# Stick-breaking attention: scan pairs counted over all rows of units, and one ScalarE gate for both heads of a step

## The chip, the cores and the metric

The program runs on one NeuronCore of a Trainium2 chip. The metric is device time in microseconds (us), the median of three runs. PE is TensorE's matmul stream and PEld its weight loads, DVE is VectorE, ACT is ScalarE, POOL is GpSimd, SP is SyncE, which here only issues DMAs.

## The reference, cut to what matters

The layer has an input projection, an mLSTM half, a stick-breaking attention half and an output projection over 4096 positions. The change touches the attention half alone, which has 8 heads of 64:

```python
z = q.k / sqrt(d)                                  # for t, s with s < t
A[t, s] = sigmoid(z_ts) * prod_{s<j<t} (1 - sigmoid(z_tj))
out[t] = sum_s A[t, s] v[s]
```

The kernel computes the gates `1 - sigmoid(z)` and their running product from the newest key to the oldest. A telescoped sum then needs only that product and differences of neighbouring values of `v` (the tensor `dw`).

## The kernel before, in words

The stage `stage_attend` works on 4 head pairs one after the other. For a pair of heads it takes the queries in 16 rows of 256 (two halves `i` of 128), from the last row (`cb` = 15) to the first (`cb` = 0). A row walks its keys in chunks of 512 from the diagonal backwards; one row and one chunk are a **unit**. The rows have 8, 8, 7, 7, 6, 6, ..., 1, 1 units, 72 per head pair and 288 in all. Within a head pair I number them 0 to 71: unit 22 is the last of row `cb` = 13, unit 23 the first of row `cb` = 12, units 66 and 67 are row `cb` = 3, 68 and 69 row `cb` = 2, 70 is row `cb` = 1, 71 is row `cb` = 0. "Unit 72" is the first of the next head pair. The first unit of a row holds the diagonal and is narrower: its halves are 384 and 512 columns wide for an odd `cb`, 128 and 256 for an even one.

For each unit:

- `scores(u)`, PE, L1329: z of both halves and both heads into four PSUM banks `a_z`; each of the 12 matmuls is 512 wide at most.
- `gates(u)`, ACT, L1426: the sigmoid from `a_z` into `a_ring`, four instructions (2 halves by 2 heads).
- the mask, POOL, L1305, for a diagonal unit.
- the scan, DVE, L1509: the running product in place in `a_ring`. Two units of a row that follow each other lie side by side in a slot of the ring, and one scan of up to 1024 columns runs over both: four scans (2 halves by 2 heads) for a pair. A row with an odd number of units ends with a pair of one, scanned 512 wide. The scan of a pair starts from the last column of the pair before. The ring has 3 slots.
- `turn(u, 0)` and `turn(u, 1)`, PE, L1345: transposes into `a_rt`, after all four scans of the pair.
- `copies(u, .)`, ACT, L1437 to L1440: `a_rt` to `a_turned`.
- `weigh(u)`, PE, L1358: the product with `dw` into `a_acc`, one unit later; `row_out`, ACT, L1450, empties it at a row's end, and SP stores the row (L1214).

Each engine works through its own fixed list and waits on semaphores. PE's list for a unit is `turn(u, 0)`, the scores of a later unit, `turn(u, 1)`, `weigh(u - 1)`; ACT's is `copies(u, 0)`, the gates of that later unit, `copies(u, 1)`. Which later unit goes by pairs: during pair p the units of pair p + 2 are scored and gated.

SP's list holds, row pair by row pair, the load of queries `a_q` for two groups of rows ahead (L1200), the stores, and the reload of the keys for the next head pair (L1206 to L1209). So the queries of unit 72 are loaded behind the store of unit 65's row and four key loads. For the last head pair two sets of loads for the next stage (L1515 to L1521) stand in that place.

Of the kernel before, what the change touches and what calls it, by code (L numbers as in the profile page):

```python
# [7 lines left out]
ALU = mybir.AluOpType  # L8
ACT = mybir.ActivationFunctionType

P = 128
# [1102 lines left out]
def stage_attend(nc, d, cols, wout_hi, wout_lo, w_out, csil, w_ada, gate_sum, b_ada, g_post, held, mix_in, o_st):  # L1114
# [34 lines left out]
    PAIRS, PAIR_OF = [], []  # L1149
    for row in range(len(LAST)):  # L1150
        for u in range(LAST[row - 1] + 1 if row else 0, LAST[row] + 1, 2):
            PAIRS.append(range(u, min(u + 2, LAST[row] + 1)))
            PAIR_OF += [len(PAIRS) - 1] * len(PAIRS[-1])

    def place(u):
        return PAIR_OF[u] % RP, 1 - (u - PAIRS[PAIR_OF[u]][0])

    with ExitStack() as ctx:
# [18 lines left out]
        z = [ps(f"z{k}", [P, CH]) for k in range(ZB)]  # L1177
# [138 lines left out]
        def _(pe):  # L1316
            def scores(u):
                hp, row, cb, j = UNITS[u]
                g = row // 2
                pe.wait_ge(q_in[g % 2], 32 * (g // 2 + 1))  # L1320
                pe.wait_ge(chunk_in[j], 64 * (hp + 1))
                for i in range(2):
                    at, w = 4 * u + 2 * i, width(u, i)
                    after(pe, keep_done, at + 2 - ZB)
                    t, s = (cb % 2 * 2 + i) * P, slice(j * CH, j * CH + w)
                    for part, (qp, k) in enumerate(((0, khi), (1, khi), (0, klo))):
                        for h in range(2):
                            e = slice(h * SD, (h + 1) * SD)
                            mm = pe.matmul(z[(at + h) % ZB][:, 0:w], q_sb[e, g % 2, qp, t:t + P], k[e, s], start=part == 0, stop=part == 2)  # L1329
                            if part == 2:  # L1330
                                mm.then_inc(z_done, 1)

            def turn(u, pair):
                k = FIRST[u] + pair
                slot, part = place(u)
                pe.wait_ge(scan_done, 4 * PAIR_OF[u] + 4)
# [41 lines left out]
            for u in range(2, PAIRS[1][-1] + 1):  # L1378
                scores(u)
            pe.wait_ge(g_act, 4)  # L1380
            for p, pair_units in enumerate(PAIRS):
                ahead = list(PAIRS[p + 2]) if p + 2 < len(PAIRS) else []
                for u in pair_units:
                    turn(u, 0)
                    if ahead:
                        scores(ahead.pop(0))
                    if blocks(u) > 2:
                        turn(u, 1)
                    if u == pair_units[-1] and ahead:
                        scores(ahead.pop(0))  # L1390
                    if u:
                        weigh(u - 1)
# [3 lines left out]
        def _(act):  # L1396
# [59 lines left out]
            for u in range(2, PAIRS[1][-1] + 1):  # L1456
                gates(u)
            for p, pair_units in enumerate(PAIRS):
                ahead = list(PAIRS[p + 2]) if p + 2 < len(PAIRS) else []
                for u in pair_units:  # L1460
                    if u >= 2:
                        row_out(u - 2)
                    copies(u, 0)
                    if ahead:
                        gates(ahead.pop(0))
                    if blocks(u) > 2:
                        copies(u, 1)
                    if u == pair_units[-1] and ahead:
                        gates(ahead.pop(0))
# [4 lines left out]
        def _(dve):  # L1474
# [21 lines left out]
            for p, pair_units in enumerate(PAIRS):  # L1496
                for s in range(4):
                    head, i = pair_units[0], s // 2
                    run = slice(0 if len(pair_units) == 2 else CH, CH + width(head, i))
                    n = run.stop - run.start  # L1500
                    dve.wait_ge(keep_done, 4 * pair_units[-1] + s + 1)
                    if diag(head):
                        dve.wait_ge(mask_done, 2 * UNITS[head][1] + i + 1)
                        first = 1.0
                    else:
                        dve.wait_ge(scan_done, 4 * p + s + 1 - 4)
                        first = ring[:, (p - 1) % RP, s, 0, 0:1]
                    line = ring[:, p % RP, s].rearrange("p a t -> p (a t)")[:, run][:, ::-1]
                    dve.tensor_tensor_scan(line, line, zeros[:, 0:1].to_broadcast([P, n]), first, ALU.mult, ALU.add).then_inc(scan_done, 1)  # L1509
# [450 lines left out]
```

## Time and profile before

| | |
|---|---|
| median of 3 runs | 3421.31 us (3420.1 to 3422.13) |
| profiled execution, its own time | 3418.25 us |
| its span, first to last instruction | 3416.5 us |
| busy: PE, DVE, ACT, POOL | 3253.6, 2420.9, 1929.0, 849.3 us |
| attention, first to last scan | 1582.4 to about 2878 us |

The busy time of an engine counts its instructions from start to end. Two instructions that follow each other overlap a little, so the distance between two starts, not the duration, says how fast an engine gets on. An idle time in brackets in the timeline stands before the instruction, with what released it. PE may be shown busy while it only advances as fast as its matmuls end.

### The profile page before, as it was taken

What the parts mean: (1) busy time and instruction counts of PE and PEld (TensorE: products, weight loads), DVE (VectorE), ACT (ScalarE), POOL (GpSimd) and SP (SyncE); (2) the same over time, 40 slices, a digit from 0 to 9 for tenths busy, and PEclk for the clock granted to TensorE, in tenths of its full rate; (3) what the DMA queues carried; (4) which work ended last, traced back from release to release, by engine and by line L of the source; (5) the groups of instructions that cost most, each with busy time, mean ns of one, the idle gap of its engine ahead of it and who ended that gap; (6) DMA issues with size and microseconds to landing.
All of it is one profiled execution on the core that took longest, in us unless ns stands there. A gap on an engine that the chain in (4) does not pass through costs nothing. (4 is left out here: it accounts for less than half of the span.)

```text
span 3416.5 us, 72847 instructions
## 1 busy us (share of the span) xinstructions
PE 3253.6 (95%) x28402; PEld 2672.1 (78%) x28402; DVE 2420.9 (71%) x2989; ACT 1929.0 (56%) x4177; POOL 849.3 (25%) x677
## 2 busy tenths in 40 slices
PE   6998999999999999997999999999999998999998
PEld 4776888999999988886776676666667666888887
DVE  4675445443578893325999999999999997666665
ACT  4553123222334452225888888888888886555554
POOL 1323332300000004422123322521252224232322
PEclk8999999999999999998999999999999999999999
DMA  8989778977955579974011201121121013566664
GB/s 293 337 311 327 257 254 308 313 237 239 320 159 189 181 251 320 319 259 139 25 34 58 62 28 44 48 67 31 40 59 50 11 33 97 177 205 200 200 205 135
DMA packets 415600, 582.65 MB, mean 171 GB/s; under 512 B 35568, under 2 KB 298096, under 8 KB 414288
## 3 DMA queue, kind: packets, MB, share of 16 engines
q1 hardware_dynamic: 394560, 506.56, 44.9%
q0 software_dynamic: 16960, 58.73, 5.1%
q10 hardware_dynamic: 3792, 13.30, 1.1%
q8 instruction: 207, 3.39, 0.4%
q14 instruction: 81, 0.66, 0.1%
HBM read 393.74 MB, written 184.75 MB: 169 GB/s over the span
## 5 line engine op out<-in xcount | busy, mean ns | idle before, releaser
L1509 DVE TENSOR_TENSOR_SCAN a_ring<-a_ring,a_zeros 128x1024 f32<-128x1024 f32 (+6 forms) x640 | 1230.9, 1998 | 67.6 <-ACT a_ring L1426 67.6
L1440 ACT COPY a_turned<-a_rt 128x512 f32<-128x512 f32 x960 | 528.3, 618 | 149.9 <-PE a_rt L1345 149.4
L1426 ACT ACTIVATE a_ring<-a_z 128x512 f32<-128x512 f32 (+3 forms) x1152 | 563.2, 602 | 3.4 <-PE a_z L1329 3.4
L1358 PE MATMUL a_acc<-a_turned,c_dw 128*64 128x256 f32 x4352 | 520.6, 380 | 7.0 <-ACT a_osum L1450 7.0
L1345 PEld LDWEIGHTS a_rt<-c_ident,a_ring 64*128 64x128 f32 x8448 | 328.0, 139 | 204.1 <-issue 95.6
L1345 PE MATMUL a_rt<-c_ident,a_ring 64*128 64x64 f32 x8448 | 370.6, 226 | 70.0 <-ACT a_turned L1440 31.6
L1305 POOL TENSOR_SCALAR_AFFINE_SELECT a_ring<-a_ring 128x256 f32<-128x256 f32 x128 | 196.8, 1552 | 893.9 <-ACT a_ring L1426 893.5
L1358 PEld LDWEIGHTS a_acc<-a_turned,c_dw 128*64 128x64 f32 x4352 | 287.4, 137 | 157.6 <-ACT a_turned L1438 9.9
L1329 PE MATMUL a_z<-c_khi,a_q 64*128 64x512 f32 (+3 forms) x2304 | 373.7, 401 | 22.9 <-DMA c_dw<-scratch_dw 12.5
L939 DVE TENSOR_TENSOR p_hlo<-p_wraw,p_hlo 128x1024 fp32r<-128x1024 f32 x85 | 104.5, 1229 | 323.2 <-ACT p_hlo L704 323.2
L704 ACT CAST p_hlo<-p_wraw 128x1024 fp32r<-128x1024 f32 x85 | 89.3, 1050 | 391.5 <-PE p_bank L572 209.5
L1329 PEld LDWEIGHTS a_z<-c_khi,a_q 64*128 64x128 f32 x2304 | 199.9, 190 | 52.3 <-issue 28.3
L1329 PE MATMUL a_z<-c_klo,a_q 64*128 64x512 f32 (+3 forms) x1152 | 224.7, 379 | 0.0
L640 POOL DMA_DIRECT2D p_hraw<-scratch_sbv x32 | 22.7, 715 | 706.5 <-DVE p_ob L1083 617.9
L939 DVE TENSOR_TENSOR p_aslot<-p_wraw,p_aslot 128x1024 fp32r<-128x1024 f32 x43 | 53.7, 1248 | 171.5 <-ACT p_aslot L704 171.3
L704 ACT CAST p_aslot<-p_wraw 128x1024 fp32r<-128x1024 f32 x43 | 45.1, 1050 | 203.3 <-PE p_bank L572 107.1
L572 PE MATMUL p_bank<-p_hhi,p_hlo 128*128 128x512 f32 x528 | 122.9, 390 | 5.2 <-DMA p_hlo<-scratch_parts 5.2
L1329 PEld LDWEIGHTS a_z<-c_klo,a_q 64*128 64x128 f32 x1152 | 113.6, 187 | 17.5
L572 PE MATMUL p_bank<-p_whi,p_hlo 128*128 128x512 f32 x528 | 123.9, 390 | 2.0 <-DMA p_hlo<-scratch_parts 2.0
L580 PE MATMUL p_bank<-p_hlo,p_whi 128*128 128x256 f32 x1008 | 124.5, 283 | 0.0
L580 PE MATMUL p_bank<-p_hlo,p_wlo 128*128 128x256 f32 x1008 | 124.4, 283 | 0.0
L1625 POOL TENSOR_TENSOR m_qs<-c_khi,m_wq 128x512 f32<-128x512 f32 x32 | 41.7, 1302 | 332.6 <-ACT m_wq L1767 328.5
(298 smaller groups left out, 6384.8 us busy)
## 6 DMA issues: line engine op xcount, KB each, us to landing
p_hlo<-scratch_parts SPq DMA_DIRECT2D x130, 512.0 KB, 5.2
p_wraw<-scratch_sums SPq DMA_DIRECT2D x128, 512.0 KB, 6.7
p_aslot<-scratch_parts SPq DMA_DIRECT2D x62, 512.0 KB, 5.0
p_u<-in_w_in POOLq DMA_DIRECT2D x64, 256.0 KB, 6.0
scratch_wsums<-p_u POOLq DMA_DIRECT2D x32, 512.0 KB, 6.5
p_hraw<-scratch_sbv POOLq DMA_DIRECT2D x32, 512.0 KB, 7.2
m_xt<-in_x SPq DMA_DIRECT2D x32, 512.0 KB, 5.1
out_y<-c_pair SPq DMA_DIRECT2D x32, 512.0 KB, 4.5
```

Source lines behind the costliest of these rows:

```text
L572: last = pe.matmul(dst[:], stationary, moving, start=fresh and k == 0 and e == 0, stop=k == 3 and e == 2, skip_group_check=True)
L580: last = pe.matmul(part, stationary, moving, start=fresh and mm == 0 and k == 0 and e == 0, stop=k == 3 and e == 2, skip_group_check=True)
L704: act.copy(a_flat[q % 3][0], araw[k % 2]).then_inc(a_hi, 1)
L939: dve.tensor_tensor(al, araw[k % 2], ah.bitcast(F32), ALU.subtract).then_inc(a_lo, 1)
L1305: pool.affine_select(out=tail, in_=tail, compare_op=ALU.is_gt, fill=1.0, base=0, pattern=[[0, 2], [-1, P]], channel_multiplier=1).then_inc ...
L1329: mm = pe.matmul(z[(at + h) % ZB][:, 0:w], q_sb[e, g % 2, qp, t:t + P], k[e, s], start=part == 0, stop=part == 2)
L1345: last = pe.transpose(rt[(2 * k + half) % RB][:, at:at + HB], ring[rows, slot, 2 * i + h, part, kb * P:(kb + 1) * P], ident[rows, rows])
L1358: last = pe.matmul(acc[h * SD:(h + 1) * SD, lo:QW], dw[:, h, j * TPC + kb, :], turned[:, (FIRST[u] + kb // 2) % TB, kb % 2, h * QW + lo:(h ...
L1426: act.activation(ring[:, slot, s, part, 0:w], z[at % ZB][:, 0:w], ACT.Sigmoid, scale=-Z_SCALE).then_inc(keep_done, 1)
L1440: act.copy(dst, src).then_inc(turned_done, 1)
L1509: dve.tensor_tensor_scan(line, line, zeros[:, 0:1].to_broadcast([P, n]), first, ALU.mult, ALU.add).then_inc(scan_done, 1)
L1625: pool.tensor_tensor(qs[:], qT[:, p], wq[:], ALU.mult).then_inc(e["qs_done"], 1)
```

## The change

Pairs are now units 2p and 2p + 1, counted over everything. Where a row ends on an even unit, the pair is made of the last unit of one row and the first of the next; it is then scanned by two scans for each half and head (`scan(u, ...)` and `scan(u + 1, ...)`), for the product must start anew. There are three such mixed pairs within each head pair (units 22 and 23, 46 and 47, 62 and 63) and a fourth at its end (70 and 71). PE and ACT now always score and gate unit u + 4 while they work on unit u. And a unit's gates are two instructions, each over both heads: `a_z` is two tensors of two banks, the semaphore `keep_done` moves by 2 when both heads are done. A gate also waits for the scan of the pair two before its own; `copies(u, 0)` ahead of it has waited for that scan already.

```diff
-    PAIRS, PAIR_OF = [], []
-    for row in range(len(LAST)):
-        for u in range(LAST[row - 1] + 1 if row else 0, LAST[row] + 1, 2):
-            PAIRS.append(range(u, min(u + 2, LAST[row] + 1)))
-            PAIR_OF += [len(PAIRS) - 1] * len(PAIRS[-1])
-
     def place(u):
-        return PAIR_OF[u] % RP, 1 - (u - PAIRS[PAIR_OF[u]][0])
+        return u // 2 % RP, 1 - u % 2
...
-        z = [ps(f"z{k}", [P, CH]) for k in range(ZB)]
+        z = [ps(f"z{k}", [P, 2, CH]) for k in range(ZB // 2)]
...
-                pe.wait_ge(scan_done, 4 * PAIR_OF[u] + 4)
+                pe.wait_ge(scan_done, 4 * (u // 2) + 4)
...
-            for p, pair_units in enumerate(PAIRS):
-                ahead = list(PAIRS[p + 2]) if p + 2 < len(PAIRS) else []
-                for u in pair_units:
-                    turn(u, 0)
-                    if ahead:
-                        scores(ahead.pop(0))
-                    if blocks(u) > 2:
-                        turn(u, 1)
-                    if u == pair_units[-1] and ahead:
-                        scores(ahead.pop(0))
-                    if u:
-                        weigh(u - 1)
+            for u in range(NU):
+                turn(u, 0)
+                if u + 4 < NU:
+                    scores(u + 4)
+                if blocks(u) > 2:
+                    turn(u, 1)
+                if u:
+                    weigh(u - 1)
...
-                if PAIR_OF[u] >= RP:
-                    act.wait_ge(rt_done, FIRST[PAIRS[PAIR_OF[u] - RP][-1] + 1])
-                for s in range(4):
-                    at, w = 4 * u + s, width(u, s // 2)
-                    act.wait_ge(z_done, at + 1)
-                    act.activation(ring[:, slot, s, part, 0:w], z[at % ZB][:, 0:w], ACT.Sigmoid, scale=-Z_SCALE).then_inc(keep_done, 1)
+                if u >= 2 * RP:
+                    act.wait_ge(rt_done, FIRST[u - 2 * RP + 1])
+                    act.wait_ge(scan_done, 4 * (u // 2 - RP + 1) + 4)
+                for i in range(2):
+                    w = width(u, i)
+                    act.wait_ge(z_done, 4 * u + 2 * i + 2)
+                    act.activation(ring[:, slot, 2 * i:2 * i + 2, part, 0:w], z[i][:, :, 0:w], ACT.Sigmoid, scale=-Z_SCALE).then_inc(keep_done, 2)
...
+            for u in range(0, NU, 2):
+                joined = UNITS[u][1] == UNITS[u + 1][1]
                 for s in range(4):
...
+                    right = CH + width(u, s // 2)
+                    if joined:
+                        dve.wait_ge(keep_done, 4 * u + 4 + s + 1)
+                        scan(u, s, 0, right).then_inc(scan_done, 1)
                     else:
...
+                        dve.wait_ge(keep_done, 4 * u + s + 1)
+                        scan(u, s, CH, right)
+                        dve.wait_ge(keep_done, 4 * u + 4 + s + 1)
+                        scan(u + 1, s, 0, width(u + 1, s // 2)).then_inc(scan_done, 1)
```

How the change moves instructions is shown at two places. The first is DVE's list around the end of row `cb` = 13 in the first head pair. The rows are the long scans over `a_ring`, with their width, and the count of equal ones; before:

```order
L1509 SCALAR_TENSOR_TENSOR a_ring<-a_ring,a_zeros 128x1024 x10
L1509 SCALAR_TENSOR_TENSOR a_ring<-a_ring,a_zeros 128x512 x4
L1509 SCALAR_TENSOR_TENSOR a_ring<-a_ring,a_zeros 128x640 x2
L1509 SCALAR_TENSOR_TENSOR a_ring<-a_ring,a_zeros 128x768 x2
L1509 SCALAR_TENSOR_TENSOR a_ring<-a_ring,a_zeros 128x1024 x8
```

And DVE's list at the same place in the changed kernel:

```order
L1492 SCALAR_TENSOR_TENSOR a_ring<-a_ring,a_zeros 128x1024 x10
L1492 SCALAR_TENSOR_TENSOR a_ring<-a_ring,a_zeros 128x512
L1492 SCALAR_TENSOR_TENSOR a_ring<-a_ring,a_zeros 128x128
L1492 SCALAR_TENSOR_TENSOR a_ring<-a_ring,a_zeros 128x512
L1492 SCALAR_TENSOR_TENSOR a_ring<-a_ring,a_zeros 128x128
L1492 SCALAR_TENSOR_TENSOR a_ring<-a_ring,a_zeros 128x512
L1492 SCALAR_TENSOR_TENSOR a_ring<-a_ring,a_zeros 128x256
L1492 SCALAR_TENSOR_TENSOR a_ring<-a_ring,a_zeros 128x512
L1492 SCALAR_TENSOR_TENSOR a_ring<-a_ring,a_zeros 128x256
L1492 SCALAR_TENSOR_TENSOR a_ring<-a_ring,a_zeros 128x1024 x12
```

Unit 22, scanned alone before, is now in one pair with unit 23, the narrow first unit of the next row, and row `cb` = 12 goes on with full pairs up to its end. Before, it began with the pair of 640 and 768 columns and ended on a pair of one.

The second place is PE's list at the end of the first head pair, from `turn(68, 0)` on (`a_rt` are transposes, `a_z` scores, `a_acc` the weighing). Before, the scores after `turn(68, 0)` are those of unit 71 (128 and 256 wide), and those of unit 72 (384 wide at first) come after `turn(70, 0)`:

```order
L1345 MATMUL a_rt<-c_ident,a_ring 128x64 x12
L1329 MATMUL a_z<-c_khi,a_q 128x128 x4
L1329 MATMUL a_z<-c_klo,a_q 128x128 x2
L1329 MATMUL a_z<-c_khi,a_q 128x256 x4
L1329 MATMUL a_z<-c_klo,a_q 128x256 x2
L1358 MATMUL a_acc<-a_turned,c_dw 64x256 x8
L1345 MATMUL a_rt<-c_ident,a_ring 128x64 x32
L1358 MATMUL a_acc<-a_turned,c_dw 64x256 x2
L1358 MATMUL a_acc<-a_turned,c_dw 64x128 x2
L1345 MATMUL a_rt<-c_ident,a_ring 128x64 x16
L1329 MATMUL a_z<-c_khi,a_q 128x384 x4
```

PE's list of the changed kernel from the same `turn(68, 0)`:

```order
L1339 MATMUL a_rt<-c_ident,a_ring 128x64 x12
L1323 MATMUL a_z<-c_khi,a_q 128x384 x4
L1323 MATMUL a_z<-c_klo,a_q 128x384 x2
L1323 MATMUL a_z<-c_khi,a_q 128x512 x4
L1323 MATMUL a_z<-c_klo,a_q 128x512 x2
L1352 MATMUL a_acc<-a_turned,c_dw 64x256 x8
L1339 MATMUL a_rt<-c_ident,a_ring 128x64 x16
L1323 MATMUL a_z<-c_khi,a_q 128x512 x4
L1323 MATMUL a_z<-c_klo,a_q 128x512 x2
L1323 MATMUL a_z<-c_khi,a_q 128x512 x4
L1323 MATMUL a_z<-c_klo,a_q 128x512 x2
L1339 MATMUL a_rt<-c_ident,a_ring 128x64 x16
```

The scores of unit 72 have moved forward by two units of work on PE, to right after `turn(68, 0)`, and those of unit 73 stand in `turn(69, .)`.

## Rows read from the trace of the kernel before

**Rows 1.** Windows, the attention: busy us (count) of each engine, clock, DMA share, GB/s

```profile
core 0: us, PE busy (x) PEld busy (x) DVE busy (x) ACT busy (x) POOL busy (x), PEclk, DMA share, GB/s
1586.00:2894.00 1308.00, 1221.49 (x16228) 891.06 (x16224) 1227.33 (x639) 1115.04 (x2488) 406.01 (x254) 1.00 0.15 45
```

**Rows 2.** Groups by shape, DVE in the attention: busy us, mean ns | idle before

```profile
L1509 DVE TENSOR_TENSOR_SCAN a_ring<-a_ring,a_zeros 128x1024 f32<-128x1024 f32 x344 | 782.4, 2344 | 9.4 <-ACT a_ring L1426 9.4
L1509 DVE TENSOR_TENSOR_SCAN a_ring<-a_ring,a_zeros 128x512 f32<-128x512 f32 x104 | 129.1, 1300 | 0.0
...
L1509 DVE TENSOR_TENSOR_SCAN a_ring<-a_ring,a_zeros 128x384 f32<-128x384 f32 x8 | 8.4, 1083 | 0.0
L1509 DVE TENSOR_TENSOR_SCAN a_ring<-a_ring,a_zeros 128x256 f32<-128x256 f32 x8 | 5.0, 659 | 0.0
L1509 DVE TENSOR_TENSOR_SCAN a_ring<-a_ring,a_zeros 128x128 f32<-128x128 f32 x8 | 3.5, 474 | 0.0
```

**Rows 3.** The tile a_ring: who waited for it, us in all and times

```profile
  DVE a_ring L1509: 67.6, 41
```

**Rows 4.** Timeline of DVE, first head pair: start, us, what, [idle before]

```profile
1582.39 42.45 DVE L1509 TENSOR_TENSOR_SCAN a_ring<-a_ring,a_zeros 128x896 f32<-128x896 f32 x20 [2.63 <-ACT a_ring L1426]
...
1685.88 6.17 DVE L1509 TENSOR_TENSOR_SCAN a_ring<-a_ring,a_zeros 128x640 f32<-128x640 f32 x4 [1.74 <-ACT a_ring L1426]
...
1718.05 33.17 DVE L1509 TENSOR_TENSOR_SCAN a_ring<-a_ring,a_zeros 128x896 f32<-128x896 f32 x16 [1.92 <-ACT a_ring L1426]
1751.38 40.87 DVE L1509 TENSOR_TENSOR_SCAN a_ring<-a_ring,a_zeros 128x1024 f32<-128x1024 f32 x20 [0.16 <-ACT a_ring L1426]
...
1907.42 53.61 DVE L1509 TENSOR_TENSOR_SCAN a_ring<-a_ring,a_zeros 128x896 f32<-128x896 f32 x25 [5.24 <-ACT a_ring L1426]
```

**Rows 5.** Timeline of DVE, the pair of units 8 and 9

```profile
1618.31 6.53 DVE L1509 TENSOR_TENSOR_SCAN a_ring<-a_ring,a_zeros 128x640 f32<-128x640 f32 x4
```

**Rows 6.** Timeline of all engines, from unit 6 to the scan of unit 10

```profile
1618.44 0.71 PE L1345 MATMUL a_rt<-c_ident,a_ring 64*128 64x64 f32 x16
...
1624.62 2.09 ACT L1426 ACTIVATE a_ring<-a_z 128x512 f32<-128x512 f32 x4
...
1625.27 2.35 DVE L1509 TENSOR_TENSOR_SCAN a_ring<-a_ring,a_zeros 128x1024 f32<-128x1024 f32 x1 [0.43 <-ACT a_ring L1426]
```

**Rows 7.** Timeline of PE, two full units

```profile
1653.32 0.71 PE L1345 MATMUL a_rt<-c_ident,a_ring 64*128 64x64 f32 x16
...
1655.90 1.95 PE L1358 MATMUL a_acc<-a_turned,c_dw 128*64 128x256 f32 x16
1657.78 0.71 PE L1345 MATMUL a_rt<-c_ident,a_ring 64*128 64x64 f32 x16
```

**Rows 8.** Groups by shape, ACT in the attention: a gate

```profile
L1426 ACT ACTIVATE a_ring<-a_z 128x512 f32<-128x512 f32 x960 | 506.4, 639 | 3.4 <-PE a_z L1329 3.4
```

**Rows 9.** Costliest groups of the page: a ScalarE operation of 1024 columns

```profile
L704 ACT CAST p_hlo<-p_wraw 128x1024 fp32r<-128x1024 f32 x85 | 89.3, 1050 | 391.5 <-PE p_bank L572 209.5
```

**Rows 10.** Timeline of PE at the end of the first head pair

```profile
1888.35 0.71 PE L1345 MATMUL a_rt<-c_ident,a_ring 64*128 64x64 f32 x16 [1.10 <-DVE a_ring L1509]
...
1896.32 0.59 PE L1345 MATMUL a_rt<-c_ident,a_ring 64*128 64x64 f32 x12
...
1902.92 0.62 PE L1329 MATMUL a_z<-c_khi,a_q 64*128 64x384 f32 x4
...
1904.23 0.56 PE L1345 MATMUL a_rt<-c_ident,a_ring 64*128 64x64 f32 x12
```

**Rows 11.** Timeline of ACT there: row_out of unit 65

```profile
1892.64 0.68 ACT L1450 ACTIVATE a_osum<-a_acc,a_v_e 128x128 f32<-128x128 f32 x2
```

**Rows 12.** Timeline of SP's queue there

```profile
1893.78 0.47 SPq L1206 DMA_DIRECT2D c_khi<-scratch_skh  x1
...
1896.21 0.43 SPq L1200 DMA_DIRECT2D a_q<-scratch_sql  x1
```

**Rows 13.** DMA issues from 1894 to 1901: KB, us from issue to landing

```profile
a_q<-scratch_sql SPq DMA_DIRECT2D x1, 256.0 KB, 4.3
```

**Rows 14.** Timeline of ACT at the end of the attention

```profile
2868.81 0.69 ACT L1450 ACTIVATE a_osum<-a_acc,a_v_e 128x128 f32<-128x128 f32 x2
...
2891.02 0.68 ACT L1450 ACTIVATE a_osum<-a_acc,a_v_e 128x128 f32<-128x128 f32 x2 [6.95 <-DMA scratch_hsb<-a_osum]
```

More of the change, by code:

```diff
@@ L1328, in scores @@
                             e = slice(h * SD, (h + 1) * SD)
-                            mm = pe.matmul(z[(at + h) % ZB][:, 0:w], q_sb[e, g % 2, qp, t:t + P], k[e, s], start=part == 0, stop=part == 2)
+                            mm = pe.matmul(z[i][:, h, 0:w], q_sb[e, g % 2, qp, t:t + P], k[e, s], start=part == 0, stop=part == 2)
                             if part == 2:
@@ L1377, in _ @@
             pe.matmul(acc[:, 2 * P:3 * P], ones[0:1, :], row(mlast_row), start=True, stop=True).then_inc(g_pe, 1)
-            for u in range(2, PAIRS[1][-1] + 1):
-                scores(u)
+            scores(2)
+            scores(3)
             pe.wait_ge(g_act, 4)
-            for p, pair_units in enumerate(PAIRS):
-                ahead = list(PAIRS[p + 2]) if p + 2 < len(PAIRS) else []
-                for u in pair_units:
-                    turn(u, 0)
-                    if ahead:
-                        scores(ahead.pop(0))
-                    if blocks(u) > 2:
-                        turn(u, 1)
-                    if u == pair_units[-1] and ahead:
-                        scores(ahead.pop(0))
-                    if u:
-                        weigh(u - 1)
+            for u in range(NU):
[6 more added lines that the diff above has]
+                    weigh(u - 1)
             weigh(NU - 1)
@@ L1455, in _ @@
             columns()
[L1456 to L1469, printed above, removed]
+            gates(2)
+            gates(3)
+            for u in range(NU):
+                if u >= 2:
+                    row_out(u - 2)
+                copies(u, 0)
+                if u + 4 < NU:
+                    gates(u + 4)
+                if blocks(u) > 2:
+                    copies(u, 1)
             row_out(NU - 2)
@@ L1495, in _, with scan @@
             dve.tensor_tensor(mprev_row[:, :, 1:NT], mlast_row[:, :, 0:NT - 1], b_before[:, :, 1:NT], ALU.add).then_inc(g_dve, 1)
-            for p, pair_units in enumerate(PAIRS):
-                for s in range(4):
[L1498 to L1504, printed above, removed]
-                    else:
[L1506 to L1509, printed above, removed]
+            def scan(u, s, left, right):
+                if diag(u):
+                    dve.wait_ge(mask_done, 2 * UNITS[u][1] + s // 2 + 1)
+                    first = 1.0
+                else:
+                    dve.wait_ge(scan_done, 4 * (u // 2) + s + 1 - 4)
+                    first = ring[:, (u // 2 - 1) % RP, s, 0, 0:1]
+                line = ring[:, u // 2 % RP, s].rearrange("p a t -> p (a t)")[:, left:right][:, ::-1]
+                return dve.tensor_tensor_scan(line, line, zeros[:, 0:1].to_broadcast([P, right - left]), first, ALU.mult, ALU.add)
+            for u in range(0, NU, 2):
+                joined = UNITS[u][1] == UNITS[u + 1][1]
+                for s in range(4):
+                    right = CH + width(u, s // 2)
+                    if joined:
+                        dve.wait_ge(keep_done, 4 * u + 4 + s + 1)
+                        scan(u, s, 0, right).then_inc(scan_done, 1)
+                    else:
+                        dve.wait_ge(keep_done, 4 * u + s + 1)
+                        scan(u, s, CH, right)
+                        dve.wait_ge(keep_done, 4 * u + 4 + s + 1)
+                        scan(u + 1, s, 0, width(u + 1, s // 2)).then_inc(scan_done, 1)
 def load_mix(sp, d, mix_in, c, p, ch_in):
```

## The prediction

> **What bounds the kernel now.** The change lies in the attention stage alone, so I read the windows over that stage first. Of 1308 us DVE is busy 1227, PE 1221, ACT 1115, POOL 406, and the granted clock is 1.00 throughout, the upper of its two levels (2.4 GHz) [rows 1]. Two engines are near full at once, so the question is which one the other waits for.
>
> The groups by shape show what DVE does: nothing but 640 scans. One of 1024 columns takes 2344 ns, one of 512 takes 1300 [rows 2]. Its idle time before scans is 67.6 us in 41 pieces, all ended by ACT's gates [rows 3]. That idle time is the most that a better order can win here; the scans themselves are fixed work.
>
> Then the timeline of DVE, to see where the idle time lies. 2.63 us come before the first scan. The rest repeats with each head pair: up to 1.74 us before the narrow pair of an even row that follows a pair of one, 1.92 before the row that comes after another such pair, a trifle of 0.16 after a narrow pair that follows full ones, and 5.24 us before the next head pair starts, where two rows of one unit each stand in front [rows 4]. Three head-pair changes at 5.24 make 15.7 us. So 67.6 - 2.6 - 15.7 = 49.3 us remain within the four head pairs, nearly all around pairs of one.
>
> Why there? PE starts to transpose a pair when its scans are done, and the gates of the pair after next come out of that same stretch of work. In [rows 6] the scans of units 6 and 7 end and PE starts at 1618.44; ACT starts the gates of unit 11 at 1624.62, and the scan of units 10 and 11 starts at 1625.27, when the first gate is there. That is 6.83 us from PE's start, about 6.88 from the end of the scan. I call it the gate delay. DVE meanwhile has one pair to scan. A full pair is 4 x 2.34 less an overlap of about 0.08 each (9.05 us): no wait. The narrow pair of units 8 and 9 takes 6.53 [rows 5], and 0.43 us of idle time come out. A pair of one takes 4 x 1.30 less overlap = 4.9, and about 2 us come out. PE itself needs 1657.78 - 1653.32 = 4.46 us for a full unit, 8.92 for two [rows 7], just under DVE's 9.0. So DVE sets the pace in the long rows, and the gate delay sets it around short pairs.
>
> **The change part by part.** *Scans.* By the lists of both kernels DVE has 640 scans again, with the same widths in sum: each row that lost a pair of one gives its 512 columns to a mixed pair, where they are still a scan of their own. Cost 0.
>
> *Mixed pairs within head pairs, 12 of them.* They take 4 x 1.30 + 2 x 0.47 + 2 x 0.66 = 7.46 us, less 8 x 0.08 = 6.8 us [rows 2]. That replaces 4.9 by 6.8 in front of the gate delay, and the rest of the row is made of full pairs.
>
> *The merged gate.* Four gates in a row take 2.09 us [rows 6] and one 0.64 [rows 8], so one advances ACT by (2.09 - 0.64) / 3 = 0.48. No gate of 1024 columns stands in the trace. Nearest is a ScalarE cast of 1024 columns, 1050 ns [rows 9]; less the 0.16 that overlaps with the next, ACT advances 0.89 instead of 0.96. 576 gates fewer give ACT about 40 us of room, worth nothing in time, since ACT has 190 us idle and isn't what paces a full pair. But the first scan of a pair now waits for both heads: 1.05 us from the gate's start instead of 0.62, so the gate delay grows by 0.43 to 7.3. The page "Perfetto Trace Analysis" of the Trainium skill, section "Optimizing Scalar/DVE Operations", says that grouping helps a saturated engine, and that where ScalarE isn't saturated but makes others wait, breaking instructions up may be better. It speaks against this half of the change, and the trace agrees in that ACT is busy only 85% of the stage while DVE waits for its gates. By its rule the merge alone would be a loss.
>
> What the delay of 7.3 leaves: after each mixed pair 7.3 - 6.8 = 0.5, twelve times 5.8 us. After the 12 narrow pairs that stay (rows `cb` = 14, 10, 6): 0.43 becomes 0.86 once, 0.16 becomes 0.6 in four, and seven with about 7.0 us of scan get 0.3 each, together 5.3 us. After full pairs there are 1.7 us of margin, and nothing is lost. So 49.3 becomes 11.1: **-38.2 us**.
>
> *Between head pairs.* Here the new order meets another wait. Unit 72's scores need queries that SP loads behind the store of unit 65's row and four key loads. `row_out` of unit 65 is at 1892.64 [rows 11], the last query load is issued at 1896.21 [rows 12] and lands 4.3 us later [rows 13], at 1900.5. PE's list had these scores at 1902.92 before, past that; now they stand behind `turn(68, 0)`, which was at 1896.32 [rows 10], and would be reached at 1896.7. SP's list and PE's up to there hold the same work, so PE will stand 3.8 us, with `weigh(67)` and `turn(69, 0)` queued behind. Then 1.3 us for the scores of unit 72 (1902.92 to 1904.23), 1.9 for weighing (1655.90 to 1657.78), 0.5 for a transpose, 0.8 for the first half of unit 73's scores: 1905.0, and 1.3 for the gate and its start: the scan starts at 1906.3, where it was 1907.42. That is 1.1 us won at each of three changes, not 5.2: **-3.3 us**. DVE's idle time there is what is left from a pair of units 70 and 71 that ends near 1902.5: 3.8 us.
>
> *The start.* The first pair's scan waits for the merged gate: **+0.4 us**.
>
> *The end.* The last row can't be emptied until SP, busy with loads for the next stage, has stored an earlier one: 2868.81 to 2891.02, with 6.95 us of ACT's wait for the DMA [rows 14]. The chain hangs on `row_out` of unit 65 and not on DVE, so the end moves with that unit, and nothing is won or lost behind it.
>
> Sum: -38.2 - 3.3 + 0.4 = -41.1 us. The profiled execution took 3418.25 us, which becomes 3377.2; the median of the runs is 3.1 us above it, which gives 3380.2. I round to **3381**.
>
> **Bounds.** If the wider gate cost the first scan no delay at all, the 11.1 would shrink to 1 and the time to 3370; if it delays by a whole second gate of 0.64, the places after short pairs cost 0.2 more each, 24 x 0.2 = 5 us: 3386. PE has 8.9 us of work per full pair against 9.0 of DVE's, so a backlog left by a mixed pair is paid back slowly; if each of the 24 places costs another 0.5, that is 12 us: 3393. Between head pairs, landing 1 us later or earlier moves 3 us in all.
>
> **The rivals.**
>
> *PE becomes the bound (chance 0.17).* For it: PE is as busy as DVE, and DVE's waits are what it used to catch up in. Against it: its idle time in the stage is 1308 - 1221 = 87 us, twice what I take away. It would show as the 12 us above, a time of 3390 to 3398.
>
> *The queries are no hindrance (0.08).* If PE didn't wait for them, the scan of unit 72 would follow 3.8 us sooner at three changes: 11 us more, 3369. Against it are the landing at 1900.5 and an unchanged list on SP.
>
> *The merge decides, slower than before (0.04).* If PE trails DVE in the long rows by more than the 1.7 us of margin, the first scan of every pair waits for the wider gate. 144 pairs x 0.43 = 62 us lost against 41 won, 3442. It decides from a delay of the gates behind the end of a full pair's scan; against it is that no scan of a full row waits now, and that ACT reaches `copies(u, 1)` 0.1 us sooner. The Trainium skill's sentence on breaking instructions up, cited above, leads here too.
>
> *It does nothing (0.03).* If the idle time only changed place, for instance a wait of 3 us behind each of 12 mixed pairs besides what is counted: 3418. Nothing speaks for it but that most orders are bound by something unseen.
>
> **How the numbers follow.** My forecast has 0.68, and its own range is 3374 to 3389. The range that leaves out 2 in 10 at most takes in half of the query case and most of the PE case: 3368 to 3396. A measurement of this kernel tells 0.2%, 7 us, from no change. Faster by more than that: 0.92; within it: 0.04; slower: 0.04.
>
> **What would show it.** DVE's idle time before scans falls from 67.6 to about 26: 3 for the start, about 0.5 behind mixed pairs, none of 1.7 to 1.9, and about 3.8 at three head-pair changes, with PE standing some 4 us before the scores of unit 72, ended by the DMA into `a_q`. Gates of 2 x 512 take 1.05 us. The time from PE's first transpose of a full pair to the scan two pairs on, where DVE waits, is 7.3 us. ACT's busy time falls, POOL's and DVE's stay, and the stages ahead and behind keep their lengths. I am wrong if scans in the long rows wait for gates, if the gate takes well over 1.1 us, if POOL's mask of unit 23 or 71 (now in the second half of its pair) holds DVE up, or if the 512-column scans in mixed pairs lose their overlap.

## The result and the profile after

| | before | after |
|---|---|---|
| median of 4 runs, us | 3420.74 (3420.1 to 3422.13) | 3394.68 (3389.24 to 3395.42) |
| profiled execution, its span, us | 3418.25, 3416.5 | 3389.24, 3387.4 |
| DVE idle before scans, us (times) | 67.6 (41) | 34.3 by tile, 34.6 by line (25) |

The ratio is 0.992, with a 95% interval of 0.9903 to 0.9937: faster, by 26 us where 40 were forecast. The profiled execution is the fastest of the four after; the other three took 5 us more, and no trace shows where. All traces, and the table at the end of this section, are of profiled executions: 29.0 us lie between them, where 41.1 were forecast. The times of the experiments are medians.

The window over the attention, with the columns of [rows 1]; its end moved from 2893.97 to 2866.34 us:

```profile
1586.00:2866.00 1280.00, 1210.75 (x16220) 891.10 (x16220) 1234.79 (x639) 1075.78 (x1916) 455.44 (x254) 0.99 0.15 46
```

Against [rows 1], ACT is busy 39 us less, and POOL 49 us more for the same 254 instructions. DVE's busy time rose, though it has 640 scans as before and as many columns in sum. The groups by line show both, scans and waits:

```profile
L1492 DVE TENSOR_TENSOR_SCAN a_ring<-a_ring,a_zeros 128x1024 f32<-128x1024 f32 (+6 forms) x640 | 1237.6, 2010 | 34.6 <-ACT a_ring L1417 28.4 <-POOL a_ring L1299 5.9
```

DVE's timeline over the first head pair, to be laid beside [rows 4]:

```profile
1626.58 61.19 DVE L1492 TENSOR_TENSOR_SCAN a_ring<-a_ring,a_zeros 128x1024 f32<-128x1024 f32 x32 [0.85 <-ACT a_ring L1417]
1687.97 61.00 DVE L1492 TENSOR_TENSOR_SCAN a_ring<-a_ring,a_zeros 128x1024 f32<-128x1024 f32 x28 [0.21 <-ACT a_ring L1417]
1749.56 42.84 DVE L1492 TENSOR_TENSOR_SCAN a_ring<-a_ring,a_zeros 128x1024 f32<-128x1024 f32 x24 [0.58 <-ACT a_ring L1417]
1792.94 42.57 DVE L1492 TENSOR_TENSOR_SCAN a_ring<-a_ring,a_zeros 128x1024 f32<-128x1024 f32 x20 [0.54 <-ACT a_ring L1417]
1835.87 53.15 DVE L1492 TENSOR_TENSOR_SCAN a_ring<-a_ring,a_zeros 128x1024 f32<-128x1024 f32 x29 [0.36 <-ACT a_ring L1417]
1890.48 5.09 DVE L1492 TENSOR_TENSOR_SCAN a_ring<-a_ring,a_zeros 128x128 f32<-128x128 f32 x7 [1.47 <-POOL a_ring L1299]
1900.92 19.74 DVE L1492 TENSOR_TENSOR_SCAN a_ring<-a_ring,a_zeros 128x896 f32<-128x896 f32 x9 [5.35 <-ACT a_ring L1417]
```

The waits of 1.7 to 1.9 us are gone; what is left within the head pair is 0.85 to 0.21. By the place in DVE's list, 0.85, 0.58 and 0.36 stand behind the three narrow pairs that stay, 0.21 and 0.54 behind the first two mixed pairs, and none behind the third. Two things are new or still there: 1.47 us in the pair of units 70 and 71, for POOL's mask of unit 71, and 5.35 before the next head pair. PE's timeline at that place answers to [rows 10]:

```profile
1893.24 0.61 PE L1323 MATMUL a_z<-c_khi,a_q 64*128 64x384 f32 x4 [3.65 <-DMA a_q<-scratch_sql]
...
1895.10 3.09 PE L1352 MATMUL a_acc<-a_turned,c_dw 128*64 128x256 f32 x16
```

PE stands 3.65 us for the queries (4.04 and 3.25 at the other two changes), as forecast. Then the weighing takes 3.09 us, where [rows 7] have 1.95. Windows over the same stretch say why; the columns are those above, and the clock is the third number from the end:

```profile
1889.50:1893.10 3.60, 0.09 (x4) 0.00 (x0) 2.62 (x4) 0.99 (x4) 1.24 (x3) 1.00 0.73 257
1893.20:1895.10 1.90, 1.86 (x12) 1.15 (x12) 1.90 (x4) 0.81 (x1) 0.00 (x0) 0.72 0.00 0
1895.10:1898.10 3.00, 3.00 (x18) 1.61 (x16) 0.47 (x1) 1.02 (x1) 1.05 (x2) 0.61 0.00 0
```

The granted clock was at its upper level up to PE's stand and through it, and at the lower one, 1.2 GHz, for some 3.4 us of what followed. At the second change the low stretch is 6.8 us long and begins 0.6 us before PE goes on; at the third it is 3.4 again. A window inside the second one:

```profile
2213.00:2216.40 3.40, 3.40 (x20) 1.90 (x18) 1.04 (x2) 1.84 (x2) 0.82 (x2) 0.50 0.00 0
```

The next table follows the scans; "within" is from the first scan to the end of the scan of units 66 and 67, in four head pairs, "between" from there to the scan of unit 72, at three changes.

| us | forecast | measured | how |
|---|---|---|---|
| start | +0.4 | +0.8 | first scan 1582.39 to 1583.19; 0.5 of it is a longer wait for the gate |
| within head pairs | -38.2 | -31.4 | 305.9 to 306.3 each, now 297.8 to 298.5; idle time -40.9, scans +9.5 |
| between head pairs | -3.3 | +3.8 | 19.1 each, now 19.95, 21.62, 19.58 |
| the end and the stage behind | 0 | -2.3 | last row's scans +0.7, from them to the end of the attention -1.6, behind it -1.4 |
| sum | -41.1 | -29.1 | |

### The profile page after: what moved, and what is told of

Same layout as the page of the kernel before. It is cut to its first block and busy times, and to the rows that moved or that the text cites. A ratio compares the mean times of both kernels' runs of the same rounds, so it can differ in the third digit from the quotient of the medians.

```text
span 3387.4 us, 72847 instructions
## 1 busy us (share of the span) xinstructions
PE 3243.9 (96%) x28402; PEld 2670.7 (79%) x28402; DVE 2427.5 (72%) x2989; ACT 1892.5 (56%) x3601; POOL 897.4 (26%) x677
## 5 line engine op out<-in xcount | busy, mean ns | idle before, releaser
L1492 DVE TENSOR_TENSOR_SCAN a_ring<-a_ring,a_zeros 128x1024 f32<-128x1024 f32 (+6 forms) x640 | 1237.6, 2010 | 34.6 <-ACT a_ring L1417 28.4
L1417 ACT ACTIVATE a_ring<-a_z 128x1024 f32<-128x1024 f32 (+2 forms) x576 | 523.8, 971 | 14.7 <-PE a_z L1323 14.7
L1299 POOL TENSOR_SCALAR_AFFINE_SELECT a_ring<-a_ring 128x256 f32<-128x256 f32 x128 | 211.1, 1665 | 815.3 <-ACT a_ring L1417 815.0
```

The costliest lines, as they stand in the source:

```text
L1299: pool.affine_select(out=tail, in_=tail, compare_op=ALU.is_gt, fill=1.0, base=0, pattern=[[0, 2], [-1, P]], channel_multiplier=1).then_inc ...
L1417: act.activation(ring[:, slot, 2 * i:2 * i + 2, part, 0:w], z[i][:, :, 0:w], ACT.Sigmoid, scale=-Z_SCALE).then_inc(keep_done, 2)
L1492: return dve.tensor_tensor_scan(line, line, zeros[:, 0:1].to_broadcast([P, right - left]), first, ALU.mult, ALU.add)
```

## The experiments

Each ratio is to the kernel before, executed alongside. **Theory**: the new order gives the gain, the merged gate costs, and what is missing is lost where the head pairs meet, at SP's queue. **Rivals**: PE or ACT has become the bound; the merge gives the gain; the masks of POOL hold DVE up; scans are longer.

### Queries ahead of the store

```
-                if g + 2 < NP * NCH:
+                if g + 2 < NP * NCH and c != 1:
                     sp.wait_ge(z_done, 4 * (LAST[row + 1] + 1))
                     load_queries(sp, g + 2)
...
+                if c == 2 and g + 3 < NP * NCH:
+                    sp.wait_ge(z_done, 4 * (LAST[row + 3] + 1))
+                    load_queries(sp, g + 3)
                 store(row + 1)
```

> The changed kernel, with one edit: the queries of the next head pair's first rows are loaded ahead of the store of unit 65's row and of the key loads behind it. Theory A (PE stands 3.3 to 4.0 us for these queries at three head-pair changes and then works at the lower of the two clock levels for a while): the DVE gaps of 5.4, 7.0 and 4.8 us fall to below 1 us each, PE's stand and the low-clock stretches there vanish, and the time falls by 14 to 18 us from the changed kernel's 3394.7, to about 3379. Rival B (the gaps are owed to the gates and to PE's backlog, the DMA is only what ends last): the gaps stay above 3 us and the time within 5 us of 3394.7.

Measured: 3376.04 us (3373.93 to 3377.88), ratio 0.9871 (0.9856 to 0.9886), 18.6 us below the kernel after (15.3 by the profiled executions) and a little more than Theory A had. PE's timeline at the first change:

```profile
1890.29 0.60 PE L1326 MATMUL a_z<-c_khi,a_q 64*128 64x384 f32 x4
...
1891.70 1.95 PE L1355 MATMUL a_acc<-a_turned,c_dw 128*64 128x256 f32 x16
```

No stand, no lower clock, and no idle time of DVE before unit 72: "between" is 14.85 us at all three changes, 16.6 less in sum than the 61.15 after. So the missing gain was in those few microseconds, and more than it: the forecast had itself reckoned with a stand. DVE's idle time in all is 17.1 us. Were PE or ACT the bound, this edit could not have given that much.

The same edit on the kernel before:

> The kernel before with the queries of the next head pair loaded early, as in the first run. Theory A (in the old order the scores of unit 72 come 2 us after the queries have landed, so nothing waits for them): no change, 3420 to 3421. Rival B (key loads and queries hinder each other or the order at the head-pair change in the old kernel too): 3 us or more faster.

Measured: 3420.11 us (3417.49 to 3425.83), ratio 1.0002 (0.9993 to 1.0011), nothing. In the old order PE came to those scores late enough; the wait for the queries belongs to the new one.

### The two halves of the change apart

Four gates a unit again, in the kernel after (the order alone), and two gates a unit in the kernel before (the merge alone):

```
-                for i in range(2):
-                    w = width(u, i)
-                    act.wait_ge(z_done, 4 * u + 2 * i + 2)
-                    act.activation(ring[:, slot, 2 * i:2 * i + 2, part, 0:w], z[i][:, :, 0:w], ACT.Sigmoid, scale=-Z_SCALE).then_inc(keep_done, 2)
+                for s in range(4):
+                    w = width(u, s // 2)
+                    act.wait_ge(z_done, 4 * u + s + 1)
+                    act.activation(ring[:, slot, s, part, 0:w], z[s // 2][:, s % 2, 0:w], ACT.Sigmoid, scale=-Z_SCALE).then_inc(keep_done, 1)
```

> The changed kernel with four gates for a unit again, so the pairing and the order alone. Theory A (the wider gate adds 0.43 us to the gate delay wherever DVE waits for it): the gaps of 0.85, 0.58, 0.54 and 0.36 us shrink by 0.4 each, the first scan starts 0.4 us sooner and each head-pair change ends 0.4 us sooner; 7 to 10 us in all, so 3385 to 3388. Rival B (fewer ScalarE instructions free the engine, and the merge is a gain of its own): slower than 3394.7, by 3 us or more.

Measured: 3389.41 us (3386.22 to 3392.97), ratio 0.991 (0.9895 to 0.9925), 5.3 us below the kernel after, a little less than Theory A had and the opposite of its rival. The profiled executions are only 1 us apart, and DVE's idle time is 32.3 us instead of 34.6.

> The kernel before with the merged gate alone, its pairing and order kept. Theory A (the wider gate lengthens the gate delay by 0.43 us at some 40 places where DVE waits for ACT): DVE's idle time grows from 67.6 to 78 to 86 us, the time from 3420.7 to between 3430 and 3438. Rival B (the merge gives ACT room and that pays): 3420 or less.

Measured: 3435.59 us (3434.51 to 3442.13), ratio 1.0048 (1.0034 to 1.0062), as Theory A had it. DVE's timeline, at the two places where [rows 4] have 1.92 and 0.16:

```profile
1720.77 33.16 DVE L1509 TENSOR_TENSOR_SCAN a_ring<-a_ring,a_zeros 128x896 f32<-128x896 f32 x16 [2.35 <-ACT a_ring L1426]
1754.53 6.83 DVE L1509 TENSOR_TENSOR_SCAN a_ring<-a_ring,a_zeros 128x1024 f32<-128x1024 f32 x3 [0.59 <-ACT a_ring L1426]
```

Both waits grew by 0.43, and the tile's row shows 87.3 us of idle time in 50 pieces against 67.6 in 41. So the merge costs 15 us in the old order and gives nothing back. In the new order, where few scans wait for a gate, it costs some 5 by the medians (3389.4 against 3394.7), which is not clear of noise, as the intervals overlap. The page "Perfetto Trace Analysis" of the Trainium skill, section "Optimizing Scalar/DVE Operations", says that a ScalarE which isn't saturated but makes others wait may do better with broken-up instructions. The runs agree: ACT is busy 85% of the stage before, and merging its gates alone cost 15 us.

Both edits together, early queries and four gates:

> The changed kernel with early queries and with four gates again. Theory A (gate delay and query wait are separate costs): 5 us less than with early queries alone (3376.0), about 3370; DVE's idle time 17.1 falls to about 12, of which 2.7 before the first scan and 5.9 for the mask of unit 71. Rival B (once nothing waits for the queries, the gates don't matter either, since what is left is PE's pace): 3376 again.

Measured: 3371.29 us (3367.68 to 3373.31), ratio 0.9854 (0.9838 to 0.9871). This is the lowest median of the study, 49 us under the kernel before and 4.7 under the one with early queries alone. DVE's idle time in it is 12.7 us in 18 pieces, 4.4 less than with early queries alone, as Theory A had it.

### What the stand does to the clock

Here PE works on 24 matmuls of 512 columns whose result nobody reads, in the place of its stand before the scores of each unit 72:

```
                 turn(u, 0)
+                if u + 4 < NU and u % 72 == 68:
+                    pe.wait_ge(keep_done, 4 * (u + 4) - 2)
+                    for _ in range(12):
+                        for h in range(2):
+                            e = slice(h * SD, (h + 1) * SD)
+                            pe.matmul(z[0][:, h, :], khi[e, 0:P], khi[e, 0:CH], start=True, stop=True)
```

> The changed kernel, with 24 matmuls of 512 columns put where PE stands for the queries of unit 72; they write the banks that the scores of unit 72 then overwrite, and change nothing of the result. Theory A (part of the cost is the lower clock level that follows the stand: weighing took 3.1 to 3.7 us there and 1.9 elsewhere): no low-clock stretch at the three head-pair changes, the gaps fall by 1.3 to 2.5 us each, and the time by 4 to 7 us, to 3388 to 3391. Rival B (the slow weighing is owed to something else at the place, such as the DMA traffic or the mask): weighing stays at 3 us and the time at 3394.7 or above.

Measured: 3389.51 us (3386.1 to 3390.42), ratio 0.991 (0.9894 to 0.9927). PE's timeline, then a window over the same place:

```profile
1895.13 0.62 PE L1323 MATMUL a_z<-c_khi,a_q 64*128 64x384 f32 x4 [0.77 <-DMA a_q<-scratch_sql]
...
1896.55 1.95 PE L1352 MATMUL a_acc<-a_turned,c_dw 128*64 128x256 f32 x16
```
```profile
1895.00:1899.00 4.00, 3.87 (x46) 2.64 (x46) 2.55 (x4) 2.18 (x4) 1.13 (x2) 1.00 0.02 4
```

The queries come no sooner (1.1 us later over the three changes), but the clock stays at 1.00 and the weighing takes 1.95. The time came out as Theory A had it. From the first of unit 72's scores to its scan it takes 6.09 us at each change, where it took 7.68, 8.96 and 7.71: 6.1 us in sum is what the low clock cost. DVE's idle time before unit 72 is 3.67, 4.23 and 4.45 us instead of 5.35, 7.01 and 4.81, which is 4.8 less, since the later queries take 1.1 back; the 12.3 that stay are the wait for the queries, where 11.4 were forecast.

### The masks of POOL

In this kernel, which has the early queries too, POOL takes its pieces of w_out's split one row earlier, so that the mask of unit 71 isn't queued behind two of them:

```
-    SPLIT_AT = ((), (0,), (1,), (2,), (3,), (4, 5), (6, 7), ())
+    SPLIT_AT = ((), (0,), (1,), (2, 3), (4, 5), (6, 7), (), ())
```

> The changed kernel with early queries, and POOL's two pieces of the w_out split that stood between the masks of units 70 and 71 done two rows sooner. Theory A (the mask of unit 71 waits behind those two on POOL's list): the four gaps of 1.47 us ended by POOL vanish; as they stand in the open now, 3 x 1.5 = 4 us less than 3376.0, so 3371 to 3373. Rival B (the gates of unit 71 are what is late): the gaps stay, ended by ACT, 3376.

Measured: 3378.98 us (3376.61 to 3380.05), ratio 0.9876 (0.986 to 0.9892), no gain, against both theories. The wait of 1.47 became 0.31, but POOL's mask now held up the pair of units 68 and 69 by 0.30, and DVE waited for the gates before unit 72, 2.07, 0.38 and 0.39 us, where it had not waited at all. The scans' busy time rose from 1237.4 to 1239.9. The wait was moved, not removed.

> Early queries, mask first and four gates on the pairing of the changed kernel. Theory A (three independent costs of 18.7, 4 and 5 us): 3366 to 3368. Rival B (PE is the bound once DVE's idle time is gone, its 8.9 us per full pair against 9.0): no better than 3371.

Measured, with the four gates as well: 3376.66 us (3374.67 to 3377.51), ratio 0.987 (0.9853 to 0.9886), 5 us above the version without that list, where Theory A had 4 below it. By the traces, the stretches within the head pairs are 7.6 us longer in sum than in that version, in waits and in the scans themselves, and the three stretches between them 2.3 shorter. So this is no sign that PE has become the bound, though the rival's number came out.

### The tail of the attention

The second of the two loads for the next stage goes behind a later store, so that ACT's last rows can be emptied:

```
-                elif c == 2:
+                elif c in (1, 2):
                     sp.wait_ge(m_out, 16)
-                    for chunk in range(2):
-                        load_mix(sp, d, mix_in, chunk, chunk, held["ch_in"])
+                    load_mix(sp, d, mix_in, 2 - c, 2 - c, held["ch_in"])
```

> As the run before, and of the two sets of loads for the next stage that SP issues ahead of the last rows' stores, the second goes behind the store of the row before the last two. Theory A (the last row's emptying waits 5 to 7 us for a store that stands behind the 14 loads): ACT's wait for that DMA vanishes and the stage ends about 5 us sooner, 3361 to 3363. Rival B (the next stage then waits for its second set of loads by as much): no change.

Measured: 3373.99 us (3373.42 to 3374.77), ratio 0.9863 (0.9847 to 0.988). From the last scan to the end of the attention it took 8.7 us instead of 15.7, as ACT's wait for the store went away. But from the last scan to the end of the program it took 537.5 instead of 537.7: the rival is right, the next stage gave the 7 us back. The total is 2.7 lower for what lies ahead of the tail, a first scan that came 1.3 us sooner and a first head pair that was 1.2 shorter.

> The changed kernel with early queries, four gates and the second set of loads for the next stage behind later stores, and POOL's list as it was. Theory A (the tail edit is worth the 2.7 us that it was worth on top of the moved POOL steps, and those steps cost 5): 3371.3 - 2.7 = 3368 to 3369. Rival B (the pieces of the split and the tail belong together): 3371 or more.

Measured: 3373.47 us (3369.19 to 3374.4), ratio 0.9863 (0.9847 to 0.988), not told apart from the best version, where Theory A had 3368 to 3369. No gain shows at this end.

### Do scans lengthen beside POOL?

Both kernels without POOL's side work. These two leave out w_out's split, the gate's partial sums and SP's reloads for them, and fill both results with ones once, early in the first head pair:

```
-    SPLIT_AT = ((), (0,), (1,), (2,), (3,), (4, 5), (6, 7), ())
-    GATE_AT = ((), (0,), (1,), (2,), (3,), (), (), ())
+    SPLIT_AT = ((), (), (), (), (), (), (), ())
+    GATE_AT = ((), (), (), (), (), (), (), ())
...
+                if u == 8:
+                    pool.memset(gate_sum[:], 1.0).then_inc(wgate_step, 1)
+                    pool.wait_ge(wgate_step, 1)
+                    for k in range(KT):
+                        pool.tensor_copy(wout_hi[:, k, :], gate_sum[:])
+                        pool.tensor_copy(wout_lo[:, k, :], gate_sum[:])
```

> The kernel before without GpSimd's side work: the slices of w_out's split and of the gate's partial sums, and SyncE's reloads for them, are left out, and both results are filled with ones once, so the output projection and the gate work on other numbers. What stays of GpSimd in the attention stage are the masks. The question is why the scans' busy time rose from 1230.9 to 1237.6 us with the change. Theory A: a scan that runs beside a GpSimd instruction takes longer (1024 wide: 2.42 us against 2.32), and the change put GpSimd's instructions beside scans where they had lain in VectorE's gaps. Then the busy time falls by a few us here (254 instructions, most of them gone, about 0.1 us each of the half that lies beside scans: 1230.9 to some 1222), and the span by 0 to 8 us, since part of the gain goes into waits for the gates. Rival B: GpSimd does nothing to the scans; busy time stays 1230.9 within 1 us, and so does the span.

> The kernel after with the same part left out (w_out's split, the gate's partial sums and their reloads). Theory A: the scans' busy time falls by more than in the kernel before, from 1237.6 to some 1224, so that the difference between the two orders shrinks from 6.7 us to 2 to 3 us or less, and the four head pairs' stretches from 298.5 us by about 2 us each; the kernel is 5 to 10 us faster than after's 3391. Rival B: a scan in the order of mixed pairs is longer by itself; the difference of the two busy times stays at 6 to 7 us and the stretches stay at 298.5 us.

Measured: the kernel before 3426.8 us (3422.79 to 3430.84), ratio 1.0017 (1.0008 to 1.0026); the kernel after 3385.4 us (3383.88 to 3387.57), ratio 0.9897 (0.9882 to 0.9912). The scans by line, of before with less POOL, and then of after with less POOL (the kernel before had 1230.9 of busy time):

```profile
L1509 DVE TENSOR_TENSOR_SCAN a_ring<-a_ring,a_zeros 128x1024 f32<-128x1024 f32 (+6 forms) x640 | 1209.3, 1964 | 93.7 <-ACT a_ring L1426 92.2 <-POOL a_ring L1299 1.5
```
```profile
L1492 DVE TENSOR_TENSOR_SCAN a_ring<-a_ring,a_zeros 128x1024 f32<-128x1024 f32 (+6 forms) x640 | 1210.6, 1966 | 52.6 <-ACT a_ring L1417 50.7 <-POOL a_ring L1293 1.5
```

The busy time falls by 21.6 and 27.0 us, and the difference between the two orders shrinks from 6.7 to 1.3. So the new order's scans are hardly longer by themselves; they are longer because POOL's instructions lie beside them. Of POOL's time, 28.4 us had no scan beside them before, and 7.4 after. The reloads by SP, which both kernels leave out too, aren't the cause: a scan of 1024 with no POOL instruction beside it takes 2.32 us with and without them. The falls are larger than the 9 and 14 us that I expected, and while the kernel after came out where Theory A had it, the kernel before was 6 us slower, against both theories.

What the shorter scans bring tells what bounds each order. In the kernel before, the scans of the second head pair up to units 66 and 67 take 7.5 us less, but the period of that head pair only goes from 325.36 (1907.42 to 2232.78) to 323.67 us: the rest came back as waits for gates, which are 93.7 in all against 67.6. In the kernel after it goes from 320.13 to 314.53, although the wait before unit 72 grew from 7.01 to 8.44: there, the scans' own length counts. The totals hide this, since my fill costs its own time: 16 casts of 1024 columns run side by side with some 17 scans, and a dozen of these take 3.05 us instead of 2.32. POOL's timeline of after with less POOL:

```profile
1636.81 3.03 POOL L1302 CAST c_wout_lo<-c_gate_sum 128x1024 fp32r<-128x1024 f32 x1
```

DVE's timeline there has five scans in 14.96 us, 3.0 each instead of 2.24. In both kernels the first head pair grew, by 10.7 and 8.3 us. That this fill alone makes the kernel before slower than it was is my reading of those two numbers; a kernel with the fill placed elsewhere was not run.

The same kernel answers whether POOL's mask of unit 71 costs anything at the head-pair changes. DVE's timeline there:

```profile
1897.70 5.09 DVE L1492 TENSOR_TENSOR_SCAN a_ring<-a_ring,a_zeros 128x128 f32<-128x128 f32 x7 [0.30 <-POOL a_ring L1293]
1910.86 10.78 DVE L1492 TENSOR_TENSOR_SCAN a_ring<-a_ring,a_zeros 128x896 f32<-128x896 f32 x5 [8.07 <-ACT a_ring L1417]
```

The wait for the mask is 0.30 instead of 1.47, and the scans of units 70 and 71 end 2.0 us sooner after those of 66 and 67. But from those to the scan of unit 72 it takes 20.70, 21.07 and 20.10 us, no less in sum than the 19.95, 21.62 and 19.58 after, with the queries' landing and the time from it to the scan each within 0.6 us in sum of what they were. As long as unit 72 waits for its queries, the wait for the mask only takes the place of a part of the wait behind it.

## Why the prediction was right, and where it was off

The direction, the main place of the gain and the range held; the size didn't: 26 us by the medians, where 40 were forecast. That the range held is in part luck. The forecast's own range ended at 3389, and the measured 3394.68 lies in the part, up to 3396, that was added for the rival in which PE becomes the bound. The runs refute that rival; what filled its place is the low clock and the longer scans below, neither of which has a term in the sum.

**What bounds the kernel.** Right: DVE sets the pace in long rows and the gate delay around short pairs. The experiment with less POOL shows it from the other side: the old order turned most of what the scans got shorter into waits.

**Within head pairs, -38.2 us.** Measured are -31.4, though the waits fell by more than computed: by 40.9. Behind the twelve narrow pairs 5.7 us are left where 5.3 were forecast (behind the first of them 0.86 and 0.85). Behind the twelve mixed pairs it is 2.4, where 5.8 were forecast. The pairs of units 46 and 47 took the 6.8 us of the forecast, and 0.54 came out behind each, where 0.5 was forecast. But those of units 22 and 23 and of 62 and 63 took 7.2 to 7.7 us, with POOL beside them, and 0.21 or nothing was left behind them. That part of the smaller waits is luck: DVE was busy instead. A gate of 2 x 512 takes 1043 ns (1050 forecast):

```profile
L1417 ACT ACTIVATE a_ring<-a_z 128x1024 f32<-128x1024 f32 x480 | 472.4, 1043 | 3.5 <-PE a_z L1323 3.5
```

**"Scans. ... Cost 0": this step was wrong.** The count and the sum of the widths are the same, and at the durations of scans with nothing beside them the change of widths is worth under 1 us. But the scans within head pairs took 9.5 us more. I counted instructions and left out what runs beside them. Of 640 scans 289 lie beside a POOL instruction and 254 did before; a scan of 1024 takes 2.32 us without and about 2.42 with one. Taking POOL's side work away took the 9.5 down to 2.1.

**"Between head pairs", -3.3 us: this step was wrong in size and sign,** +3.8. PE's stand was right (3.8 forecast; 3.65, 4.04 and 3.25 measured), and so was the landing (4.3; 4.0, 4.8 and 4.0). The forecast and the measurement are 7.1 us apart, and all but 0.2 of it lies behind the landing: from the first of unit 72's scores to its scan the prediction has 1.3 + 1.9 + 0.5 + 0.8 + 1.3 = 5.8 us, and it took 7.68, 8.96 and 7.71. The cost that was missing is the clock. It was at its lower level there, so that "1.3 us for the scores" and "1.9 for weighing" were twice as slow in part. With the stand filled the same stretch takes 6.09 at each change, so of the 7.1 us the clock's part is 6.1, and 0.9 are steps that I had set too short. POOL's mask of unit 71, which the prediction names as a way to be wrong, did hold DVE up by 1.47 in each head pair, but at the three changes that cost nothing, as the kernel with less POOL showed. With early queries nothing hides it any more: the wait stands there with none behind it.

**The merged gate.** The rule of the Trainium skill held, and so did my price of 0.43 for the first scan, in the old order; with early queries, four gates are 4.7 us faster than two. The gate of 2 x 512 took what was forecast. The rival in which the merge decides failed: it costs 15 us alone, and the order more than pays for it.

**The start and the end.** +0.8 against +0.4, and -2.3 against 0; both are small, and the tail's experiments show no gain from shortening the end.

**The rivals.** PE didn't become the bound: within a head pair DVE is busy 295 of 298 us, and early queries could not have won 18.6 us otherwise. Queries *were* a hindrance, and the case in which they are none is the version of the first experiment: 3376, where I put 3369. Open are the 5 us between the profiled execution and the other three runs of the kernel after.

## What to carry to other kernels

A reordering that removes stalls also moves an engine's start towards transfers that were hidden until then: look in the DMA queue for what stands ahead of the next load, and move the load with the order. Here one load moved in SP's list was worth 18.6 us, some 70% of what the whole change gave, and nothing without the change. A reordering that closes an engine's gaps also takes away the time in which another engine worked undisturbed. And a wait in a trace is a cost only if nothing behind it waits for something later. Merging instructions on an engine that isn't saturated but is waited for cost, in both orders, the time by which the first result came later; test each half of a double change alone.

## What the runs showed of the hardware

**PE's stands of 3.3 to 4.0 us cost twice.** Behind them the granted clock was 0.50 for 3.4 us twice and for 6.8 us once, and 16 matmuls of 256 columns took 3.09 to 3.68 us instead of 1.95. With the stands filled down to 0.77, 1.33 and 1.55 us the clock stayed at 1.00. The other kernels bear it out: with the order alone and in the kernel after with less POOL, all eight stands of 3.1 to 4.9 us come with a low stretch. Shorter ones are not always safe: of seven stands of 1.8 to 1.9 us, with the merge alone and with the mask first, two were followed by one of 3.4 us.

**Scans and POOL's instructions lengthen each other.** POOL's same 254 instructions took 406 us before and 456 after, where less of their time fell into DVE's gaps. The scans' busy time is 21.6 and 27.0 us less without the side work. Where casts of 1024 columns run without a pause, scans and casts go on at the same pace, one of each in 3.0 us. The page "SBUF — State Buffer" of the Trainium skill describes, in its section "Who interferes with whom", a port pair that VectorE and GpSimd share as an exclusive lock, and has a VectorE operation with two inputs in SBUF contend with a GpSimd one that reads SBUF. The common pace of 3.0 us agrees with it, but whether one waits there for the whole of the other isn't shown, as no cast of 1024 ran without a scan beside it. Elsewhere POOL loses more than DVE: in the kernel before, a cast of 256 columns took 0.39 us where DVE stood and 1.62 on average, while a scan of 1024 loses 0.1 us on average beside a POOL instruction.
